# Query tiles of the prompt attention in one order for all head pairs: 0, 1, 6, 7, 2, 3, 4, 5

## What is computed

```python
SEQ, N_HEADS, QK_HEAD_DIM, V_HEAD_DIM, Q_BLOCK = 1024, 8, 96, 64, 128

def block(args):                      # 128 queries of every head
    qb, start = args
    s = jnp.einsum('bqhd,bkhd->bhqk', qb, k) * scale
    q_pos = start + jnp.arange(Q_BLOCK, dtype=jnp.int32)
    s = jnp.where(key_pos[None, :] <= q_pos[:, None], s, -jnp.inf)
    p = jax.nn.softmax(s, axis=-1)
    ctx = jnp.einsum('bhqk,bkc->bqhc', p, ckv_f)
    return jnp.einsum('bqhc,chv->bqhv', ctx, w_uv_f)
```

## Time and profile before

| | |
|---|---|
| Time, median of 3 runs | 2204.19 us (2203.75 to 2207.69) |
| The profiled execution's own time | 2206.78 us |
| Its span, first to last instruction | 2205.0 us |
| `attend_prompt`, PE's first score to its last mixing | 242.5 to 399.8 us of the span |
| PE busy over the whole span | 98% |
| Mean granted TensorE clock over the span | 0.991 of full speed |

### The profile page before, as it was taken

How to read it: one execution, slowest core, us unless ns; L and a number is a source line. 1 busy time by engine, 2 the same in 40 slices (tenths; PEclk the granted TensorE clock), 3 DMA queues, 4 the chain that set the end, 5 groups by cost and what they waited for, 6 DMA issues and landing times.

```text
span 2205.0 us, 33853 instructions
## 1 busy us (share of the span) xinstructions
PE 2151.8 (98%) x12537; PEld 1800.3 (82%) x12537; DVE 1528.8 (69%) x2353; ACT 971.1 (44%) x2273; POOL 702.2 (32%) x765
## 2 busy tenths in 40 slices
PE   8999899999999999999999989999999999999999
PEld 7987566788787878787878768799999999977776
DVE  4447776688888878887878775666767676644344
ACT  5445575556565656565656552312111111233333
POOL 2554110467565757574747352100000000000000
PEclk9999999999999999999999999999999999999999
DMA  5310100342222222222323032221111111044353
GB/s 171 59 29 1 61 24 12 106 155 90 89 91 88 93 87 94 84 96 75 106 73 120 34 120 96 82 77 40 46 48 48 48 48 48 19 176 150 132 185 125
DMA packets 95811, 183.20 MB, mean 83 GB/s; under 512 B 9416, under 2 KB 65568, under 8 KB 87311
## 3 DMA queue, kind: packets, MB, share of 16 engines
q1 hardware_dynamic: 79933, 96.53, 13.5%
q0 software_dynamic: 15744, 84.93, 11.3%
HBM read 167.39 MB, written 14.36 MB: 82 GB/s over the span
## 4 chain that ended last, share of the span: by engine, by line
PE 78%; DVE 2%; issue 1%; ACT 0%; POOL 0%; ACTq 0%; DVEq 0%; POOLq 0%
PE ca_banks L1785 31%; PE ca_banks L2393 22%; PE ca_banks L2666 11%; PE ca_banks L1761 5%; PE ca_banks L1845 5%; PE ca_banks L1797 3%; PE ca_banks L2642 0%; DVE ca_cells L2242 0%; DVE ca_lo L2118 0%; DVE ca_cells L2237 0%; PE ca_banks L1876 0%; DVE ca_room L2504 0%; DVE ca_down_lo L2706 0%; PE ca_banks L1828 0%; PE ca_banks L1887 0%
## 5 line engine op out<-in xcount | busy, mean ns | idle before, releaser
L2033 ACT ACTIVATE ca_banks<-ca_banks 128x512 f32<-128x512 f32 x512 | 298.2, 582 | 325.4 <-PE ca_banks L1785 320.7
L1785 PE MATMUL ca_banks<-cache_w_hi,ca_hi 128*128 128x512 f32 x1024 | 427.9, 418 | 6.5 <-DVE ca_lo L2118 5.8
L2237 DVE TENSOR_REDUCE ca_cells<-ca_banks 128x8 f32<-128x512 f32 x512 | 352.3, 688 | 88.8 <-ACT ca_banks L2033 73.6
L1785 PE MATMUL ca_banks<-cache_w_lo,ca_hi 128*128 128x512 f32 x1024 | 403.2, 394 | 0.0
L1785 PE MATMUL ca_banks<-cache_w_hi,ca_lo 128*128 128x512 f32 x1024 | 401.8, 392 | 0.0
L1785 PEld LDWEIGHTS ca_banks<-cache_w_hi,ca_lo 128*128 128x128 f32 x1024 | 193.2, 189 | 46.6
L1785 PEld LDWEIGHTS ca_banks<-cache_w_hi,ca_hi 128*128 128x128 f32 x1024 | 193.1, 189 | 44.9 <-DVE ca_lo L2118 10.8
L1785 PEld LDWEIGHTS ca_banks<-cache_w_lo,ca_hi 128*128 128x128 f32 x1024 | 193.8, 189 | 32.4
L1651 POOL TENSOR_TENSOR ca_product<-cache_kpe,attn_q_row_odd 128x512 f32<-128x512 f32 x128 | 164.7, 1290 | 172.3 <-DVE ca_cells L2242 170.8
L2118 DVE TENSOR_TENSOR ca_lo<-ca_banks,ca_hi 128x512 fp32r<-128x512 f32 x256 | 175.1, 684 | 56.7 <-ACT ca_hi L1936 56.2
L1651 POOL TENSOR_TENSOR ca_product<-cache_kpe,ca_q_row_even 128x512 f32<-128x512 f32 x128 | 164.8, 1295 | 131.5 <-DVE ca_cells L2242 130.2
(11 more groups left out here) (400 smaller groups left out, 4319.0 us busy)
## 6 DMA issues: line engine op xcount, KB each, us to landing
ca_down_raw<-in_w_down SPq DMA_DIRECT2D x44, 512.0 KB, 3.3
keep_w_uv<-in_w_gate SPq DMA_DIRECT2D x22, 512.0 KB, 3.8
ca_up_raw<-in_w_up SPq DMA_DIRECT2D x22, 512.0 KB, 3.6
keep_ctx<-in_w_down SPq DMA_DIRECT2D x22, 512.0 KB, 3.5
late_room<-in_x_prompt SPq DMA_DIRECT2D x8, 512.0 KB, 3.6
ca_m<-mixed_scratch SPq DMA_DIRECT2D x8, 512.0 KB, 5.3
ca_w_raw<-in_w_o SPq DMA_DIRECT2D x16, 256.0 KB, 2.5
ca_x<-in_x_prompt SPq DMA_DIRECT2D x8, 512.0 KB
```

Of the source, the lines that this page charges most:

```text
L1785: last = nc.tensor.matmul(KK[:, t, :], x[:, n % 2, t, ck, :], w[:, par, ck, :], start=(m == 0), stop=(m == 5))
L2033: nc.scalar.activation(SQ[:, t, :], KK[:, t, :], ACT.Square).then_inc(squared, 1)
L2237: nc.vector.tensor_reduce(ss[:, par, 2 * n + t, :], SQ[:, t, :].rearrange("p (h d) -> p h d", d=DN), AX.X, ALU.add).then_inc(summed, 1)
```

## The change

The order of the tiles is the same for all four head pairs: 0, 1, 6, 7, 2, 3, 4, 5. So the items come in groups of four: four small ones (tiles 0 and 1), four large ones (6 and 7), four small ones (2 and 3), four large ones (4 and 5). The number of items that are scored before the first `turn` is worked out in another way, since item 4 is now a large one whose banks were held by items 0 and 1; that number is 4 both before and after. Nothing else is changed: the same instructions are issued for each item, and the preparations stay at their item numbers.

```diff
-        items = [(hp, PT - 1 - i if hp % 2 else i, e) for hp in range(NH // 2) for i in range(PT)
-                 for e in range(2)]
+        TURNS = (0, 1, 6, 7, 2, 3, 4, 5)
+        items = [(hp, i, e) for hp in range(NH // 2) for i in TURNS for e in range(2)]
...
-            issued = before.index(0)
+            issued = next(n for n in range(len(items)) if before[n] >= 0)
```

## The result

The changed kernel takes 2211.87 us (median of 5 runs, 2210.3 to 2215.39), the kernel before 2205.43 us (5 runs as well, 2203.75 to 2207.69). The ratio is 1.0033, 95% interval 1.0022 to 1.0044. So it is slower by 6.4 us between the medians and by 7.3 us by the ratio, beyond the 2208.5 us at which the forecast range ended.

A forecast was written before the change was run, and what follows sets the result against it. PE, with its waits, was taken to bound the kernel. Terms +0.1 (pair 0), -1.2 (pairs 1 to 3) and -0.9 (preparations) gave -2.0: 2206.8 to 2204.8, less 2.6 for the median, 2202.2 us; range 2196.5 to 2208.5.

The forecast's parts named there:

- PE's own work: Attention stage: PE's scores, transposes, mixing and preparations priced by spacing, 128.5 us, the same before and after.
- the clock's 5.7 us: Attention stage: cost of the stretches at half clock, some 5.7 us, with all three falls kept.
- the 23 us of waits before: Attention stage before, 157.3 us: about 23 us PE waits, 7.6 of them among the small items around tile 0.
- The start: Items 0 and 1 go as before; item 4's 1.49 us of scores run at half clock; `score(6)` is reached at 254.45.
- The wait at item 14: Fall to the next pair's tile 0: `turn(14)` waits 1.1 us for DVE, which is in `peak(15)`.
- pairs 1 to 3: 107.1 before, 105.9 after: Head pairs 1 to 3 less preparations: 107.1 us before, 105.9 after from 3 x 35.1 and the last mixing; -1.2 us.
- The preparations: "a", after item 42 just ahead of the rise: its 3.8 us hide that wait and part of the next; -0.9 us.
- The pair: One head pair in the new order: 4.3 to 4.4 us of PE waits, so it takes 35.1 us.
- The end: End of the stage: the last mixing has nothing behind it; PE's last mixing should end near 398 us.
- The valley's loss: Rival, small items around tile 0: PE is fed all the time, the 7.6 us loss goes, 2196.2 us; chance 0.20.
- The full wait for the output copy at every fall: Rival, seven falls: each costs a full wait, 1.23 us, walked as 0.2 to 0.3; net +4.9, 2209.1 us; chance 0.12.
- The clock did not fall at the falls: Rival: PE's waits of 1.1 and 0.5 us, close together three times, lower the clock; +4.8, 2209.0 us; chance 0.06.

The follow-up runs named there:

- after_w_early: The new order with the four "w" preparations moved to items 0 to 3; ratio 1.0019 against the kernel before.
- after_scale_first: The new order with DVE scaling items 14, 30, 46 and 62 ahead of the next item's maximum; ratio 1.0061 against the kernel before.
- after_all_three: The new order with "w" at items 0 to 3, copies first at falls, and scaling first at items 14, 30, 46, 62; ratio 1.0040 against before.
- after_last_pair_down: The new order in pairs 0 to 2, with pair 3 in descending order, tiles 7 to 0, as before; ratio 1.0028 against the kernel before.
- after_snake: The new order with pairs 1 and 3 taking the tiles backwards (5, 4, 3, 2, 7, 6, 1, 0); ratio 1.0014 against the kernel before.

## Why the prediction was wrong

**What held.** PE's own work, the clock's 5.7 us and the 23 us of waits before are the ledger's 128.8, 5.8 and 22.5. The start went as walked: `score(6)` came at 255.06, walked for 254.45, in a stage that now began 0.65 later. The wait at item 14 (walked 1.1, measured 1.04), those before `turn(6)` (0.4, 0.35) and at the next rise (0.3 and 0.45, against 0.31 and 0.40 by spacing) are there. The large mixing does hide small items, and copies of item 7 are covered by `mix(2)`.

**The step that failed is the sum "pairs 1 to 3: 107.1 before, 105.9 after"**, which I gave as -1.2 us, and -0.9 for the preparations. The last mixing ended at 407.6, walked for 398.5 (with the later start), 9.1 us sooner. By the ledger it is waits that were too few, some 21 us forecast and 30.0 measured. Three terms of it:

- The preparations, about 4.7 us. I took off 5.6 us of own work before, but not the waits around them, and walked the new pairs without any. These waits are in both orders: 2.7 us before and 2.4 after, as the moved "w" shows, and 1.48 at "q" in the new order, behind item 38 with its late copies (0.31 before). I wrote that "w" waits for copies in both orders and then left it out of one side. "a" waits 0.31 us against 0.69, but the pair around it lost only some 0.3 us of other waits where I had taken off 0.9.
- The pair, 3 to 4 us. I walked 35.1 us; it is 36.1 in after_w_early. `turn(15)` waits 0.8 rather than 0.5, and hand-overs make up most of the rest. I had such differences in the bounds in both signs. Single ones did have both (the 0.2 and 0.3 us for the output ahead of the second mixings came out as 0.05), but over four pairs the sum has one sign.
- The end, about 0.5 us. I let the last pair end like any other. PE waits 1.6 and 0.8 us in the last two turns by spacing, against 1.04 and 0.81 at the same items of the first pair.

The clock was no part of the miss: it cost 5.3 us where I had 5.7. It was low under the last mixing, which I had not, but the low stretch behind "a" was half as long.

That accounts for the distance to my walk. The loss against before is another sum, and the preparations drop out of it (3.8 us of waits before, 4.2 after): it is made in the pairs, 2.1, 2.3, 1.1 and 0.9 us, and at the start, 0.8.

**The rivals.** The valley's loss did not go. The full wait for the output copy at every fall is not what happened: the second mixing waits little, and it is turns and preparations that wait, for DVE and for copies behind an exponential. But its size, 2209.1 us and slower, was the nearest of my figures, and I had given it 0.12. The clock did not fall at the falls of this kernel; with a longer gap there it fell at three of six. That the new order is slower even with its faults mended was in none of my cases: I had taken the valley's 7.6 us for something a mixed order could only share. But large items next to large ones lost nothing that the exponentials show (13.65 us of work in 13.63), and breaking up such runs is what the new order does.

## What to carry to other kernels

Where a pipeline with a fixed program on each engine runs without gaps among equal items, alternating big and small items to balance engines by the sum can cost more than it hides: at a fall the look-ahead work of PE shrinks at once, while the other engines are still behind with large items, as the 1.04 and 0.81 us at items 14 and 15 show. When comparing orders, take waits out of both sides by the same cut, or measure one order with the disputed work moved away. Before changing the order, look for work placed badly in it: here two edits of one line each gave 0.26%, and a new order none.

## What the runs showed of the hardware

A gap of PE does not by itself decide whether the clock falls. At the falls to tile 0, gaps of 1.04 us for DVE (alone, or with a second one of 0.5 to 0.8 close behind) left the granted clock at 1.00 at all 14 places in five kernels. One gap of 1.70 us in the same place was followed by a fall at three of six: the first and second in after_scale_first (0.83 over 4 us), the second in after_all_three (0.72 over 6 us), not the other three. The wait of 1.48 us ahead of "q" was followed by one at two of five (after_last_pair_down, after_scale_first). The Trainium skill (TensorE: Matmul & The Clock Gate, section A second HAM failure mode: psum-queue depth-cycling) tells of short, frequent idle times between groups of matmuls that made the clock swing in a bfloat16 kernel. The traces here agree for some of the longer gaps and disagree for the shorter ones, which come only once or twice in a head pair.

The falls differ between executions of one kernel, and the time with them: of the 27 executions of the kernel before that were timed beside after_snake, one had a mean granted clock of 0.994 and took 2203.26 us, another 0.990 and 2209.51 us.

Weight load time is no better a measure of room than matmul time in this stage, with its float32 scores of up to 512 columns. From 262 to 292 us before, PE was busy without a gap, and the eight-block items there took no more time than their price by spacing (13.63 us against 13.65). Loads were busy for 19.93 of the 30 us.
